# Hybrid step kernel: sampled attention in another order, first transfers split and the parameters sent behind the pages, y stored by tiles

## What is computed

```python
def nsa_attend(q, gates, q_pos, ctx, kw, vw, w_pos):
    ...
    g = gates.astype(o_c.dtype)
    return g[..., 0:1] * o_c + g[..., 1:2] * o_s + g[..., 2:3] * o_w
...
def layer_tail(x, mix, ffn_prev, p, ln_mg, ln_mb, ln_fg, ln_fb, w_up, conv_w, conv_b, w_down, w_proj, w_gate):
    h = layer_norm(ALPHA * x + mix, ln_mg, ln_mb)
    f, ffn_state = conv_ffn(h, ffn_prev, w_up, conv_w, conv_b, w_down)
    h = layer_norm(ALPHA * h + f, ln_fg, ln_fb)
    return h + jax.nn.sigmoid(h @ w_gate) * (p @ w_proj), ffn_state
```

## Time and profile before

| | us |
|---|---|
| median of three runs | 1640.69 (1639.3 to 1641.22) |
| the profiled execution's own time | 1640.43 |
| its span, first to last instruction | 1638.8 |
| PE busy | 1579.2 (96% of the span) |
| DVE, ACT, POOL busy | 1000.2, 722.3, 322.6 |
| first matmul starts | 7.75 |
| last operation on y starts | 1621.32 |
| store of y issued | 1622.40 |
| HBM read, written | 140.57 MB, 9.10 MB |

### The profile page before, as it was taken

The page is one execution under the profiler, slowest core; times in us unless marked ns, Lnnn a source line. Parts: engine busy times, 40 slices in busy tenths (PEclk is TensorE's granted clock), DMA queues, the critical chain, the costliest instruction groups (busy, mean ns, idle before and its releaser), DMA issues.

```text
span 1638.8 us, 31404 instructions
## 1 busy us (share of the span) xinstructions
PE 1579.2 (96%) x12538; PEld 1541.5 (94%) x12538; DVE 1000.2 (61%) x1576; ACT 722.3 (44%) x1316; POOL 322.6 (20%) x742
## 2 busy tenths in 40 slices
PE   8999899988999999999999999999999999999995
PEld 8999777868999999999999998999999999999995
DVE  3346687775787345535567786868863554355582
ACT  4445677863444334313435437634542342234250
POOL 4711344520054012102200000002620220122000
PEclk9999999999999999999999999999999999999998
DMA  7645000043122322222221322231322222222221
GB/s 267 140 113 208 1 1 1 17 169 113 66 89 82 101 78 91 91 79 89 91 102 65 100 82 72 94 121 52 103 83 98 78 91 91 87 83 101 91 74 59
DMA packets 41483, 148.00 MB, mean 90 GB/s; under 512 B 6305, under 2 KB 8369, under 8 KB 40897
## 3 DMA queue, kind: packets, MB, share of 16 engines
q1 hardware_dynamic: 35568, 123.35, 23.2%
q0 software_dynamic: 5776, 22.71, 4.0%
HBM read 140.57 MB, written 9.10 MB: 91 GB/s over the span
## 4 chain that ended last, share of the span: by engine, by line
PE 87%; DVE 6%; ACT 3%; issue 2%; DMA 0%; POOL 0%; ACTq 0%; DVEq 0%
PE PS L2025 75%; PE PS L2187 2%; PE PS L2149 2%; PE PS L2063 2%; PE PS L2064 2%; ACT ARENA L836 1%; PE PS L2320 1%; DVE SMALL L1348 1%; PE PS L2139 1%; PE PS L2140 1%; DVE LO L472 1%; DVE X L1641 1%; PE PS L2173 1%; ACT HI L466 0%; DVE ARENA L1724 0%
## 5 line engine op out<-in xcount | busy, mean ns | idle before, releaser
L2025 PE MATMUL PS<-XH,HI 128*128 128x272 f32 (+1 forms) x1936 | 405.7, 291 | 10.4 <-DVE XL L1192 8.5
L2025 PE MATMUL PS<-XH,LO 128*128 128x272 f32 (+1 forms) x1936 | 401.4, 289 | 0.0
L2025 PE MATMUL PS<-XL,HI 128*128 128x272 f32 (+1 forms) x1936 | 400.4, 288 | 0.0
L466 ACT ACTIVATE HI<-RAW 128x1024 fp32r<-128x1024 f32 x223 | 235.2, 1057 | 256.5 <-PE PS L2025 232.4
L472 DVE TENSOR_TENSOR LO<-RAW,HI 128x1024 fp32r<-128x1024 f32 x223 | 274.1, 1230 | 106.4 <-ACT HI L466 106.1
L2025 PE MATMUL PS<-GH,HI 128*128 128x272 f32 (+1 forms) x1504 | 315.6, 291 | 5.5 <-ACT ARENA L1113 3.5
L2025 PEld LDWEIGHTS PS<-XH,HI 128*128 128x128 f32 x1936 | 306.4, 189 | 12.3 <-DVE LO L472 8.5
L2025 PE MATMUL PS<-GH,LO 128*128 128x272 f32 (+1 forms) x1504 | 311.4, 289 | 0.0
L2025 PE MATMUL PS<-GL,HI 128*128 128x272 f32 (+1 forms) x1504 | 311.0, 288 | 0.0
L2025 PEld LDWEIGHTS PS<-XL,HI 128*128 128x128 f32 x1936 | 304.9, 188 | 0.1
L2025 PEld LDWEIGHTS PS<-XH,LO 128*128 128x128 f32 x1936 | 303.7, 188 | 0.0
(11 more groups left out here) (375 smaller groups left out, 1906.2 us busy)
## 6 DMA issues: line engine op xcount, KB each, us to landing
RAW<-in_w_stream SPq DMA_DIRECT2D x223, 512.0 KB, 3.3
ARENA<-in_cache_cmp POOLq DMA_DIRECT2D x32, 128.0 KB, 3.1
out_win_old<-in_win_copy POOLq DMA_DIRECT2D x1, 4064.0 KB, 18.3
X<-in_x SPq DMA_DIRECT2D x4, 544.0 KB, 7.4
X<-in_x POOLq DMA_DIRECT2D x1, 2176.0 KB, 8.2
out_y<-X POOLq DMA_DIRECT2D x1, 2176.0 KB, 6.9
ARENA<-in_cache_sel POOLq DMA_DIRECT2D x16, 128.0 KB, 2.5
ARENA<-in_cache_win POOLq DMA_DIRECT2D x4, 512.0 KB, 4.8
```

The costliest lines, as they stand in the source:

```text
L466: nc.scalar.activation(HI[:, s * CH:(s + 1) * CH], RAW[:, (c % RAWS) * CH:(c % RAWS + 1) * CH], ACT.Copy).then_inc(hi_ready, 1)
L2025: ins = mm(PS[0:rows, b + h, 0:width], w[:, 0:rows], cols(part, h), start=first and len(parts) == 2 and n == 0, stop=last and len(parts) == 1)
```

## The change

It does three things, one for each place.

**Start.** Of chunk 0 the first 256 columns come in a transfer of their own (`w_first`), then x tiles 0 and 1 in one each, the other 768 columns, and three transfers of two x tiles; ACT and DVE split chunk 0 in the same two pieces. The first tile of w_in waits for the pieces that each k needs. PE first runs eight matmuls of 128 columns on zeros (`zeros_ready`). The parameters are issued behind the 32 pages.

**Sampled attention.** `sample_max` reduces the scores first and waits for the small scores only then; block 0's maxima no longer stand behind the copies into `LATER` and the clearing of `PMS2[0]` (now at unit 50). `out_hi(15)` stands ahead of `sample_exps(1)`. The copy of `PTM2` moves from DVE to ACT. Splits of w_out's chunks, scales, sums and copies stand in another order on ACT and DVE, and PE does `sample_values(2)` ahead of `sample_trans(3)`, and `sample_values(3)` ahead of `sample_turn(0)`.

**End.** The last tile of gate 1 is computed half by half, and its sigmoid and its two DVE operations are done per half. SP stores y: seven tiles of 272 KB, each when it is ready, and two halves of the eighth.

The diff (counts of semaphores and their declarations left out):

```diff
@@ -495,10 +498,12 @@
-            load(0, 0)
-            for i in range(4):
-                cols = slice(2 * i * TOK, 2 * (i + 1) * TOK)
+            sp.dma_start(RAW[:, 0:2 * P], W[0:P, 0:2 * P]).then_inc(w_first, 16)
+            for i, (k0, k1) in enumerate(((0, 1), (1, 2), (2, 4), (4, 6), (6, 8))):
+                cols = slice(k0 * TOK, k1 * TOK)
                 sp.dma_start(X[:, cols], a["x"][:, cols]).then_inc(x_landed[i], 16)
+                if i == 1:
+                    sp.dma_start(RAW[:, 2 * P:CH], W[0:P, 2 * P:CH]).then_inc(raw_landed[0], 16)
             load(1, 1)
@@ -529,18 +534,30 @@
+            def store(c0, c1):
+                sp.dma_start(outs["y"][:, c0:c1], X[:, c0:c1]).then_inc(y_out, 16)
...
+            for k in range(KT - 1):
+                sp.wait_ge(y_ready, KT + k + 1)
+                store(k * TOK, (k + 1) * TOK)
+            sp.wait_ge(y_half, 1)
+            store((KT - 1) * TOK, (KT - 1) * TOK + HALF)
+            sp.wait_ge(y_ready, 2 * KT)
+            store((KT - 1) * TOK + HALF, KT * TOK)
+            sp.wait_ge(y_out, 16 * (KT + 1))
...
             pool.dma_start(PAGE[:, :], a["pages"]).then_inc(page_landed, 16)
-            pool.dma_start(PAR[:, :], a["params"]).then_inc(par_landed, 16)
             pool.wait_ge(page_landed, 16)
...
                 pool.dma_start(CR[:, n, :], a["cache_cmp"][bass.ds(pg * P, P), :]).then_inc(cmp_landed, 16)
+            pool.dma_start(PAR[:, :], a["params"]).then_inc(par_landed, 16)
@@ -675,9 +692,7 @@
             tail(1, 4)
-            pool.wait_ge(y_ready, 16)
-            pool.dma_start(outs["y"], X[:, :]).then_inc(out_dma, 16)
-            pool.wait_ge(out_dma, 96)
+            pool.wait_ge(out_dma, 80)
@@ -685,10 +700,14 @@
             splits = Splits(act, split_hi)
-            split_hi(act, 0)
+            act.wait_ge(w_first, 16)
+            s.activation(HI[:, 0:2 * P], RAW[:, 0:2 * P], ACT.Copy).then_inc(first_hi, 1)
             for k in range(KT):
-                act.wait_ge(x_landed[k // 2], 16)
+                act.wait_ge(x_landed[k if k < 2 else k // 2 + 1], 16)
                 s.activation(XH3[:, k, :], X3[:, k, :], ACT.Copy).then_inc(in_hi, 1)
+                if k == 1:
+                    act.wait_ge(raw_landed[0], 16)
+                    s.activation(HI[:, 2 * P:CH], RAW[:, 2 * P:CH], ACT.Copy).then_inc(hi_ready, 1)
             for c in (1, 2):
@@ -893,6 +912,7 @@
                     act.wait_ge(pv_done, 16 + v - 1)
+                chain.did(s.activation(PTM2[v % 2][0:96], probs_t(v), ACT.Copy))
                 s.activation(PT2[v % 2][:, 1, :], PS[:, 5, :], ACT.Copy).then_inc(pt_act, 1)
@@ -901,15 +921,17 @@
             sample_exps(0)
+            out_hi(15)
             sample_exps(1)
-            out_hi(15)
             sample_copy(0)
...
             sample_exps(2)
+            splits.cap = C0["w_out"] + 1
+            splits.after(O0["w_out"] - 1)
+            sample_copy(2)
             sample_exps(3)
...
             splits.after(O0["w_out"] - 1)
-            sample_copy(2)
             sample_copy(3)
@@ -1072,6 +1094,13 @@
                     o = O0[f"gate{layer}"] + k
+                    if layer == 1 and k == 7:
+                        act.wait_ge(y_ready, 14)
+                        act.wait_ge(last_half, 1)
+                        s.activation(LT[:, TOK:TOK + HALF], banks(o)[:, 0, :], ACT.Sigmoid).then_inc(last_gate, 1)
+                        act.wait_ge(tile_done, o + 1)
+                        s.activation(LT[:, TOK + HALF:2 * TOK], banks(o)[:, 1, :], ACT.Sigmoid).then_inc(act_took, 1)
+                        continue
                     act.wait_ge(tile_done, o + 1)
@@ -1191,11 +1220,18 @@
-            split_lo(dve, 0)
+            v.memset(HS[:, 0:P], 0.0).then_inc(zeros_ready, 1)
+            dve.wait_ge(w_first, 16)
+            dve.wait_ge(first_hi, 1)
+            sub_lo(LO[:, 0:2 * P], RAW[:, 0:2 * P], HI[:, 0:2 * P], first_lo)
             for k in range(KT):
-                dve.wait_ge(x_landed[k // 2], 16)
+                dve.wait_ge(x_landed[k if k < 2 else k // 2 + 1], 16)
                 dve.wait_ge(in_hi, k + 1)
                 sub_lo(XL3[:, k, :], X3[:, k, :], XH3[:, k, :], in_lo)
+                if k == 1:
+                    dve.wait_ge(raw_landed[0], 16)
+                    dve.wait_ge(hi_ready, 1)
+                    sub_lo(LO[:, 2 * P:CH], RAW[:, 2 * P:CH], HI[:, 2 * P:CH], lo_ready)
             for c in (1, 2):
@@ -1430,6 +1466,8 @@
                     out_lo(n - 2)
+                if u == 50:
+                    chain.did(v.memset(PMS2[0], 0.0))
                 if u < 62:
@@ -1447,17 +1485,20 @@
                 dve.wait_ge(s_done, 65 + x // 2)
...
+                w0 = PS[:, 2 * (u % 2) + 1, 0:4]
+                chain.did(v.tensor_tensor(w0, w0, SMASK[:, 4:8], ALU.add))
+                chain.sync()
+                chain.did(v.tensor_reduce(nm[:, 1:3], PS[:, 2 * (u % 2):2 * (u % 2) + 2, :], AX_X, ALU.max, negate=True))
                 if x >= 2:
                     dve.wait_ge(pt_done, transposed(u - 1))
...
-                w0 = PS[:, 2 * (u % 2) + 1, 0:4]
-                chain.did(v.tensor_tensor(w0, w0, SMASK[:, 4:8], ALU.add))
+                else:
+                    dve.wait_ge(small_done, 4)
                 chain.did(v.tensor_copy(pms[:, 0:32], mb[:, 0:32]))
...
                 chain.did(v.memset(pms[:, NC:NC + 1], NEG))
-                chain.did(v.tensor_reduce(nm[:, 1:3], PS[:, 2 * (u % 2):2 * (u % 2) + 2, :], AX_X, ALU.max, negate=True))
                 chain.did(v.tensor_reduce(nm2, pms[:, 160:480].rearrange("p (r c) -> p r c", r=2)[:, :, 0:4], AX_X, ALU.max,
@@ -1468,7 +1509,6 @@
                     dve.wait_ge(pv_done, 16 + x - 1)
-                chain.did(v.tensor_copy(PTM2[x % 2][0:96], probs_t(x)))
                 v.tensor_copy(PT2[x % 2][:, 0, :], PS[:, 4, :]).then_inc(pt_dve, 1)
@@ -1501,31 +1541,33 @@
+            sample_max(0)
             dve.wait_ge(small_done, 4)
...
                 chain.did(v.tensor_copy(LATER[x], small_scores(2 + x)))
-            for x in range(2):
-                chain.did(v.memset(PMS2[x], 0.0))
-                chain.sync()
-                sample_max(x)
+            chain.did(v.memset(PMS2[1], 0.0))
+            chain.sync()
+            sample_max(1)
             out_lo(15)
...
             sample_copy(1)
+            sample_scales(0)
+            sample_sum(0)
             sample_max(3)
-            sample_scales(0)
+            splits.cap = C0["w_out"] + 1
+            splits.after(O0["w_out"] - 1)
+            sample_copy(2)
             sample_scales(1)
-            sample_sum(0)
             sample_sum(1)
...
             splits.after(O0["w_out"] - 1)
-            sample_copy(2)
             sample_scales(2)
...
             sample_scales(3)
+            sample_sum(2)
             splits.cap = N_CHUNKS
             splits.after(O0["w_out"] - 1)
-            sample_sum(2)
             sample_out_lo(0)
@@ -1837,6 +1879,15 @@
                     lt = LT[:, (k % 2) * TOK:(k % 2 + 1) * TOK]
+                    if layer == 1 and k == 7:
+                        for h, (gate, at, done) in enumerate(((last_gate, 1, y_half), (act_took, taken(o)[1], y_ready))):
+                            dve.wait_ge(gate, at)
+                            chain.did(v.tensor_tensor(half(PP3[:, k, :], h), half(PP3[:, k, :], h), half(lt, h), ALU.mult))
+                            chain.sync()
+                            v.scalar_tensor_tensor(out=half(X3[:, k, :], h), in0=half(X3[:, k, :], h),
+                                                   scalar=par(f"ln_fb{layer}", k), in1=half(PP3[:, k, :], h),
+                                                   op0=ALU.add, op1=ALU.add).then_inc(done, 1)
+                        continue
                     dve.wait_ge(act_took, taken(o)[1])
@@ -2015,17 +2066,17 @@
-            def products(o, c, k, xh, xl, x, first, last, rows=P, width=HALF):
+            def products(o, c, k, xh, xl, x, first, last, rows=P, width=HALF, hs=(0, 1), done=tile_done):
...
                     for n, part in enumerate(parts):
-                        for h in range(2):
+                        for h in hs:
                             ins = mm(PS[0:rows, b + h, 0:width], w[:, 0:rows], cols(part, h),
...
                 if last:
-                    ins.then_inc(tile_done, 1)
+                    ins.then_inc(done, 1)
@@ -2036,9 +2087,22 @@
-            for n in range(15):
-                tile(n, C0["w_in"] + n, range(KT), XH3, XL3, 0, rows=48 if n == 6 else P,
-                     each=(lambda k: pe.wait_ge(in_lo, k + 1)) if n == 0 else None)
+            pe.wait_ge(zeros_ready, 1)
+            for n in range(8):
+                mm(PS[:, 7, 0:P], HS[:, 0:P], HS[:, 0:P], start=True, stop=True)
...
+            def first_tile(k):
+                if k < 2:
+                    pe.wait_ge(first_lo, 1)
+                else:
+                    chunk_ready(0)
```

(17 more changed lines are left out.)

7 lines of the change are left out of this document (5 added, 2 removed).

## The result

The changed kernel takes 1627.38 us (median of four runs, 1626.24 to 1629.27); the kernel before, on the same chip, 1640.88 (1639.3 to 1641.22).

A forecast was written before the change was run, and what follows sets the result against it. PE, busy for 1579.2 of 1638.8 us, was taken as the bound; end -5.8, start -1.7 and sampled attention +1.5 sum to -6.0, from 1640.43 to 1634.4, stated as 1634.5 at the median's level; range 1631.5 to 1638.0.

The forecast's parts named there:

- the constant: Kernel's end: the 9.5 us behind the last store's landing hold no instruction and stay, with 1 allowed either way.
- Store: Kernel's end: the last 136 KB of y land in 2.1 us in place of 6.9, a gain of 4.8.
- Rival A: Last store: its time is not in its bytes, the end gains only 1.0, total 1639.4; chance 0.09.
- Halves: Last tile: sigmoid and two DVE operations on 272 columns take 1.22 us in place of 2.21, a gain of 1.0.
- Start: First tiles of w_in: tile 1 starts at 14.65 in place of 16.4, -1.7 us; gain bounds 0.8 and 2.6.
- PE's start at 5.7: Start: less data ahead and shorter splits let PE's first matmul begin at about 5.7 us.
- The bandwidth: Start: transfers run at about 410 GB/s, so the bytes ahead of a piece set when it lands.
- the 402 KB of parameters: Start: issued behind the pages, they no longer precede chunk 1, whose bytes come 1.0 us earlier.
- Sampled attention: Stage before w_out: the new order costs +1.5 us, bounds +0.2 and +4.5.
- the chain: Sampled attention: block 3's exponentials behind block 2's copy, w_out starting at about 380.4 in place of 379.29, +1.1 us.
- A fall of the clock behind w_out's start: Around w_out's start: a further clock fall, 1.7 us, at about one in four, +0.4 as a mean.
- Rival B: Sampled attention costs nothing and the first tile runs at full clock, -8.2 in all, 1632.4; chance 0.19.

The follow-up runs named there:

- e3: The changed kernel, with POOL also waiting at the end of its list for SP's last store and issuing nothing; 1636.04 us in one run.
- e15: The changed kernel, with POOL's last wait made one for the seventh tile of y, nothing issued behind it; 1632.03 us in one run.
- e4: The changed kernel, with the first half of y's last tile stored by POOL in place of SP; 1635.08 us in one run.
- e2: The changed kernel, with its nine stores of y moved from SP's list to the end of POOL's; 1638.89 us, ratio 0.9991.
- e1: The kernel before, with only the whole of y stored by SP in one transfer in place of POOL; 1629.98 us, ratio 0.9938.
- e10: The changed kernel with the old sampled attention, and POOL issuing the pages only once chunk 1 has landed; 1625.26 us, ratio 0.9916.
- e11: The kernel before with the end changed, and pages, then parameters, issued only once chunk 1 has landed; 1625.95 us, ratio 0.9924.
- e14: The changed kernel, with ACT's exponentials of block 3 back ahead of w_out's first split and block 2's copies; 1624.96 us in one run.
- e16: The kernel before with only the end changed (last tile by halves, y stored by tiles and halves by SP), run again; 1623.99 us, ratio 0.9896.
- e12: The changed kernel with the old sampled attention and without the eight matmuls on zeros; 1624.97 us in one run.
- e5: The changed kernel with the sampled attention as it was before; 1625.64 us, ratio 0.9909.

## Why the prediction was wrong

**The step that failed is the constant.** "The other 9.5 us to the span's end hold no instruction; I take them as a constant", with 1 allowed either way. They hold POOL's drain, 9.14 us long, and it follows POOL's last wait whoever moves the data (e3) and shifts with that wait (from it to the span's end 9.5 in e15, 9.6 in e4, 10.2 in e2). By giving SP the store the change let POOL's list end at about 1511, and 9.1 of the 9.5 went; SP's end takes the 0.4 that are left. The prediction had named that POOL's list would end earlier and SP's later, and put a price of 1 on it with the words "no row shows it". A row did: the trace of the kernel before has POOL's drain with 9140 ns beside SP's with 129, on the line that ends the lists. And even without that row the bound was the stretch itself: 0 to -9.5. With that the forecast would have been 1634.5 or 1625, and the range would have held the time. The 1 that was allowed is in neither end of the range as it was given (-8.9 and -2.6).

**Store.** Forecast 2.1 for 136 KB, measured 1.7 (SP) and 2.0 (POOL): right, as was the whole's 6.9 (6.6 by SP). Rival A is refuted: the store's time was in its bytes. The five microseconds that tiles add to e1 are in the tails, 7.0 and 2.1. **Halves.** Forecast 1.0, measured 0.8 (1.40 for 2.21).

**Start.** Forecast -1.7, measured +0.1 in this pair and +0.7 over all profiles. PE's start at 5.7 was nearly right (6.16, bounded as said by x tile 0). Two terms failed. The bandwidth was taken as 410 with the new pieces too; from 2 to 8 us it was 284 GB/s, which costs 1.3, and x tile 2 came so late that PE stood idle for 2.3 us; half the clock followed, and tile 1 began at 16.6, not at 14.65. And the 402 KB of parameters were credited with 1.0, of which the pages took about half (0.2 MB fewer on POOL's queue, 0.5 us by bytes); the text knew that they might and gave that its bound, 0.8. Both together put chunk 1 at 13.74 in place of 12.2 and the truth outside the bounds. The late pages of e10 and e11 confirm the rest of the working, that bytes ahead of chunk 1 set it.

**Sampled attention.** Forecast +1.5 with +1.1 of it in the chain; measured +2.1 in the pair, +1.75 on average, inside the bounds. The mechanism is right by e14: the exponentials of block 3 stand behind block 2's copy. Two of its parts were off in size: putting the exponentials back gains 3.2, not 1.1 (2.3 at the same clock), since the rest of the new order saves 1.4 (0.6 at the same clock) that the prediction said was given back. A fall of the clock behind w_out's start did come, 1.7 us in this profile; it is part of the +0.7 in the table's fourth row. It was given one chance in four: it came in all six profiles with the new order, but also in four of nine with the old one. Rival B, by which the new order costs nothing, is refuted by the stage; that the time went past its 1632.4 is the constant's doing.

**What was in no term.** The stretch from the mark to POOL's issue of x, on which the change does nothing to speak of, was 2.5 shorter. Over twenty profiles of all kernels it was 326.7 to 331.0, of both starts and orders alike. It goes with the clock that was granted over it: in the three shortest (326.7 to 327.5; e16, e2, e11) that reads 1.00, in the five longest (330.4 to 331.0; e12, before, e5, e4, e14) 0.98, in the changed kernel 0.99. The falls differ from execution to execution. That is luck, and it makes one profiled execution a poor witness for a term of 1 us.

The account: -9.1 for the constant, +1.8 for the start, +0.6 for the stage, -2.5 for the stretch without a term, +1.7 behind w_out's start (+0.7 where -1.0 was forecast, the fall of the clock above all), and -0.7 in the store itself (0.4 in its landing, 0.3 since SP issues it at once), give -8.2 between forecast and profile, -6.0 and -14.2.

## What to carry to other kernels

Time behind the last landing is a cost with an owner: look at the rows of the line that ends the lists, which no timeline shows, for the engine whose drain ends last. End POOL's list early (here its last wait had to be over 7.4 us before DVE's last operation was), whether or not it moves data at the end; where it can't end early, each transfer that another engine issues in its place should save 0.08, an estimate from the drains behind 110, 111 and 119 transfers. Split the first transfers only if the window's GB/s hold; and what stands in an engine's list ahead of an operation that PE waits for must be ready earlier than that operation's own input. Where an idle stretch has no explanation, its whole length is the bound, not a margin of one.

## What the runs showed of the hardware

- POOL's list takes 9.4 to 10.2 us from its last wait to the end of the span (e2, e3, e4, e15 and before), also with no transfer of its own in flight; SP's takes some 0.4 (e1). 9.06 to 9.79 of it are POOL's drain, which is 0.0823 us for each transfer that POOL issued in the whole kernel (110, 111, 119), whatever its size and however long ago it landed. What POOL does for each of them no row shows.
- Tiles of 272 KB land 4.3 us after SP's issue and 2.3 after POOL's (e2), pieces of 136 KB 1.7 and 2.0. No run tells why the first pair differs so much; beside matmuls it costs nothing.
- A burst of matmuls on zeros of 3.4 to 3.8 us, ended 0.8 to 1.3 us before the first real matmul, left the clock at full in four of ten profiles and not in six. In the changed kernel, one of the four, PE then waited for 2.3 us, and about 1 us behind that wait the granted clock fell to half.
